# One fused two-layer kernel: modulation work respread over the merge, small chains moved under the projections, scores negated

## What is computed

```python
# block 1
h = rms_norm(x, norm_gain);  proj = h @ w_in
q, kv_all, g_nsa, br_gate, u_lru, g_lru, merge_g = split(proj)
#   NSA mixer: compress_blocks(kv) -> kc, vc (31 blocks);  softmax(q @ kc + bias) @ vc,
#   plus two causal attentions (q @ k + bias, softmax, @ v), gated and summed
#   RG-LRU mixer: causal conv of u, two block-diagonal sigmoid gates, a linear scan over time
m = sigmoid(gate_a) * (y_a @ w_proj_a) + sigmoid(gate_b) * (y_b @ w_proj_b)
x = x + m @ w_out
# block 2, its start
mod = c @ w_ada + b_ada                        # c: 1024 numbers, w_ada: 1024 x 6144
shift1, scale1, gate1, shift2, scale2, gate2 = split(mod)
h = rmsnorm(x) * (1 + scale1) + shift1         # and so on: mLSTM, differential attention, 32 experts
def compress_blocks(kv, pe, w1, b1, w2): return silu(blocks(kv, pe) @ w1 + b1) @ w2
```

## Time and profile before

| | |
|---|---|
| median of 3 runs | 1457.43 us (1455.88 to 1460.79) |
| the profiled execution: its time | 1454.09 us |
| its span, first to last instruction | 1452.2 us |
| PE busy | 1285.8 us (89%) |
| DVE busy | 519.4 us (36%) |
| ACT busy | 311.1 us (21%) |
| POOL busy | 148.4 us (10%) |
| mean granted clock of TensorE | 0.936 |
| DMA | 208.73 MB |

### The profile page before, as it was taken

The page is one execution under the profiler, slowest core; times in us unless marked ns, Lnnn a source line. Parts: engine busy times, 40 slices in busy tenths (PEclk is TensorE's granted clock), DMA queues, the critical chain, the costliest instruction groups (busy, mean ns, idle before and its releaser), DMA issues.

```text
span 1452.2 us, 12168 instructions
## 1 busy us (share of the span) xinstructions
PE 1285.8 (89%) x4480; PEld 612.9 (42%) x4480; DVE 519.4 (36%) x1391; ACT 311.1 (21%) x729; POOL 148.4 (10%) x150
## 2 busy tenths in 40 slices
PE   7998879999958899999999986999999779777774
PEld 3454334445523344664444444444444533222221
DVE  2015483667377612222722357110103333222221
ACT  3111643333200001222322343200001211111110
POOL 6000023344200000000000000000000012111101
PEclk9999999999979999999989997999999769899897
DMA  9413321332275212331310110014123659999982
GB/s 307 92 58 66 116 81 36 117 116 88 87 249 185 87 41 76 116 116 60 114 58 0 59 58 1 0 58 174 58 93 143 269 196 372 410 410 408 405 332 34
DMA packets 90815, 208.73 MB, mean 144 GB/s; under 512 B 19913, under 2 KB 50905, under 8 KB 78423
## 3 DMA queue, kind: packets, MB, share of 16 engines
q1 hardware_dynamic: 77344, 186.79, 35.0%
q0 software_dynamic: 10064, 17.96, 5.0%
q10 hardware_dynamic: 3344, 3.16, 0.7%
HBM read 203.60 MB, written 12.66 MB: 149 GB/s over the span
## 4 chain that ended last, share of the span: by engine, by line
PE 65%; DVE 13%; DMA 11%; ACT 4%; issue 3%; SPq 2%; POOL 1%; DVEq 0%; ACTq 0%; POOLq 0%
DMA AN<-in_w_up 8%; PE PS L1993 8%; PE PS L1408 8%; PE PS L1508 6%; PE PS L932 5%; PE PS L2337 5%; PE PS L2003 4%; PE PS L1553 4%; DVE AN L1205 4%; PE PS L588 3%; PE PS L1332 3%; SPq L2251 2%; PE PS L1520 2%; PE PS L1791 2%; PE PS L658 2%
## 5 line engine op out<-in xcount | busy, mean ns | idle before, releaser
L932 PE MATMUL PS<-HT,W 128*128 128x512 f32 x256 | 128.6, 627 | 3.5 <-ACT AN L1096 3.2
L1993 PE MATMUL PS<-HT,W 128*128 128x512 f32 x256 | 113.7, 597 | 0.0
L2337 PE MATMUL PS<-AN,HT 128*64 128x512 f32 x272 | 99.0, 716 | 14.6 <-DMA AN<-in_w_up 14.6
L1408 PE MATMUL PS<-W,AN 128*128 128x512 f32 x256 | 111.0, 592 | 0.9 <-DVE AN L2039 0.9
L2337 PE MATMUL PS<-W,HT 128*64 128x512 f32 x240 | 83.6, 656 | 27.0 <-DMA AN<-in_w_up 16.6
L1191 POOL TENSOR_SCALAR AN<-AN,SM 128x128 f32<-128x128 f32 (+3 forms) x64 | 71.8, 1131 | 186.1 <-DVE SM L1276 186.1
L1508 PE MATMUL PS<-W,HT 128*128 128x512 f32 x192 | 87.0, 612 | 0.0
L1205 DVE SCALAR_TENSOR_TENSOR AN<-AN,COLA 128x256 f32<-128x256 f32 x168 | 84.0, 500 | 5.8
L2286 POOL DMA_INDIRECT AN<-scr_xn,SM x16 | 16.6, 1040 | 616.4 <-DVE SM L2163 609.3
L1993 PEld LDWEIGHTS PS<-HT,W 128*128 128x128 f32 x256 | 49.1, 192 | 61.6 <-issue 61.6
L1408 PEld LDWEIGHTS PS<-W,AN 128*128 128x128 f32 x256 | 48.2, 190 | 60.5 <-issue 58.8
(11 more groups left out here) (434 smaller groups left out, 1694.2 us busy)
## 6 DMA issues: line engine op xcount, KB each, us to landing
W<-in_w_in SPq DMA_DIRECT2D x14, 2048.0 KB, 7.9
AN<-in_w_ada SPq DMA_DIRECT2D x17, 1024.0 KB, 5.2
AN<-in_w_gate SPq DMA_DIRECT2D x17, 1024.0 KB, 21.2
AN<-in_w_up SPq DMA_DIRECT2D x17, 1024.0 KB, 29.7
W<-in_w_gate SPq DMA_DIRECT2D x15, 1024.0 KB, 19.8
W<-in_w_up SPq DMA_DIRECT2D x15, 1024.0 KB, 29.7
AN<-in_w_down SPq DMA_DIRECT2D x12, 1024.0 KB, 18.5
W<-in_w_down SPq DMA_DIRECT2D x10, 1024.0 KB, 16.9
```

Source lines behind the costliest of these rows:

```text
L932: t = pe.matmul(u.ap, w[:, c, tile(m)], hT[:, c, :], start=c == 0, stop=c == 7)
L1408: t = pe.matmul(u.ap, src[:, c, tile(i)], wv(slots[n], 8, 512)[:, c, :], start=c == 0, stop=c == 7)
L1993: t = pe.matmul(u.ap, w[:, c, tile(mh)], hT[:, c, :], start=c == 0, stop=c == 7)
L2337: t = pe.matmul(u.ap[r, :].rearrange("p (n f) -> p n f", n=2), XGT[e % 2][:, c, r], w_gu(3 * e + half)[:, c], start=c == 0, stop=c == 7)
```

## The change

Four things are changed; no arithmetic is added or taken away but the negations.

1. **Modulation in the merge.** The 34 half parts are spread over merge steps 0 to 27 (`ada_step`), where each of steps 0 to 16 had two. The PE sums take banks 6 and 7 in turn, and three sum buffers are used, so a part's first chunk waits for the sum of three parts ago.
2. **Modulation in attention.** A part is done by 2 chunks in each of 4 steps (it was 4 chunks in each of 2 steps), and its load is issued as two halves of 512 KB by POOL. Its PE sum and its read-out come later.
3. **Start-up.** The raw keys' and values' transposes (`pe_blocks`), `dve_st`, the scalar chains and the clearing move up behind the bias stage, under the `q` projection; the compression is cut into three pieces, which stand between the tiles of the `u` projection; weights of `kw` and `u` swap slots 2 and 3, so that the loads of `gn` can start earlier; `kcT` goes ahead of the gates. In attention steps 0 to 3 the LRU's ACT work goes behind the score exponential.
4. **Negated scores.** Queries are scaled by -0.125 and the bias table is negated, the maximum becomes a minimum, and ACT's exponential has scale -1.0 with the minimum itself as bias. The negation L1256 falls away (64 times).

The core of the diff:

```diff
@@ act_bias
-            act.activation(B2[:, 2 * j:2 * j + 2, :].rearrange("p h k -> p (h k)"), u.ap, ACT.Copy).then_inc(*u.read)
+            act.activation(B2[:, 2 * j:2 * j + 2, :].rearrange("p h k -> p (h k)"), u.ap, ACT.Copy, scale=-1.0).then_inc(*u.read)
@@ sp_kvq
-        sp.dma_start(wv(2, 8, 280)[:, :, 0:256], wsrc(w1in, 1024, 256)).then_inc(*ring[2].up("kw"))
...
-        sp.dma_start(wv(3, 8, 512), wsrc(w1in, 1816, 512)).then_inc(*ring[3].up("u"))
+        sp.dma_start(wv(3, 8, 280)[:, :, 0:256], wsrc(w1in, 1024, 256)).then_inc(*ring[3].up("kw"))
...
+        sp.dma_start(wv(2, 8, 512), wsrc(w1in, 1816, 512)).then_inc(*ring[2].up("u"))
@@ pe_gates
+        u = B.take(0, 8, "kcT")
+        wp.wait_ge(*u.free)
+        wp.wait_ge(*cmp_dve.at("kcn"))
+        pe.transpose(u.ap[:, 0:31], KCN[0:31, :], ident[0:31, 0:31]).then_inc(*u.filled)
         for m in range(4):
@@ sp_attention
-        ws.wait_ge(*B.use("u", 3).full)
+        ws.wait_ge(*B.use("kw", 3).full)
...
-        ws.wait_ge(*B.use("cmp", 1).full)
+        ws.wait_ge(*B.use("hid").full)
@@ pe_ada
-        a = ACC[p % 2]
-        u = B.take(6, 7, "ada", p)
+        a = ada_sum(p)
+        u = B.take(6, 7, "ada", p) if p < ATT_PARTS else B.take(6, 8, "ada", p)
@@ pe_attention
-            if p is not None and r == 3:
-                pe_ada(pe, wp, p)
+            if r == 2 and 0 < p <= ATT_PARTS:
+                pe_ada(pe, wp, p - 1)
@@ act_attention
-            act_lru(act, wa, step)
+            if step >= 4:
+                act_lru(act, wa, step)
...
-                wa.wait_ge(*max_dve.at("neg", step))
-                act.activation(PU[step % 5][:, 0:n], b.ap[:, 0:n], ACT.Exp, bias=MXA[:, 2 * step + 1:2 * step + 2],
+                wa.wait_ge(*max_dve.at("max", step))
+                act.activation(PU[step % 5][:, 0:n], b.ap[:, 0:n], ACT.Exp, bias=MXA[:, 2 * step:2 * step + 1], scale=-1.0,
                                accum_out=SMA[:, step:step + 1]).then_inc(*b.read)
+            if step < 4:
+                act_lru(act, wa, step)
@@ pool_attention
+            p, half = divmod(step - 34, 4)
+            if 0 <= p < ATT_PARTS and half in (0, 2):
+                wg.wait_ge(*(ada_dve.at(p - 1, 3 + 2 * half) if p else lru_dve.at("y", 3)))
+                pool.dma_start(STAGE[0].rearrange("p (c n) -> p c n", c=8)[:, 2 * half:2 * half + 4],
+                               wada[:, 2 * half:2 * half + 4, 256 * PARTS[p]:256 * PARTS[p] + 256]).then_inc(*part_in[half // 2].up(p))
@@ dve_ada
+    def ada_sum(p):
+        return ACC[p % 2] if p < ATT_PARTS else (ACC + [TY[:, 0:256]])[p % 3]
+
+    def dve_ada(dve, wd, p, lo, hi):
...
+        for c in range(lo, hi):
+            if c % 4 == 0:
+                wd.wait_ge(*(part_in[c // 4].at(p) if p < ATT_PARTS else stage_in[s].at(p)))
             if c == 0:
-                wd.wait_ge(*(part_in.at(p) if p < ATT_PARTS else stage_in[s].at(p)))
-                wd.wait_ge(*(B.use("ada", p - 2).full if p > 1 else av_pe.at(12)))
+                if p < 2:
+                    wd.wait_ge(*av_pe.at(12))
+                elif p == 8:
+                    wd.wait_ge(*B.use("acc", 3).full)
+                else:
+                    wd.wait_ge(*B.use("ada", p - 2 if p < 8 else p - 3).full)
@@ dve_attention
-            if p is not None and r < 2:
-                dve_ada(dve, wd, p, r)
-            if p is not None and r == 3:
-                dve_mod(dve, wd, p)
+            if r == 3 and 0 < p <= ATT_PARTS:
+                dve_mod(dve, wd, p - 1)
+            if 0 <= p < ATT_PARTS:
+                dve_ada(dve, wd, p, 2 * r, 2 * r + 2)
...
                 dve.tensor_tensor_reduce(b.ap[:, lo:n], b.ap[:, lo:n], B2[:, h, 256 - (n - lo):256], 1.0,
-                                         m2 if lo else -3e38, ALU.add, ALU.max, mx).then_inc(*max_dve.up("max", step))
-                wd.wait_ge(*max_dve.at("max", step))
-                dve.tensor_scalar(m2, mx, -1.0, None, ALU.mult).then_inc(*max_dve.up("neg", step))
+                                         m2 if lo else 3e38, ALU.add, ALU.min, mx).then_inc(*max_dve.up("max", step))
@@ merge
+    def ada_step(p, half):
+
+        return (2 * (p - ATT_PARTS) + half) * 14 // (24 - ATT_PARTS)
+
     def pe_merge1(pe, wp):
         for step in range(3, 32):
             if step not in (4, 5):
                 pe_merge1_part(pe, wp, step)
-            if step < 20:
-                pe_ada(pe, wp, ATT_PARTS + step - 3)
+            for p in range(ATT_PARTS, 24):
+                if step == ada_step(p, 1) + 3:
+                    pe_ada(pe, wp, p)
@@ dve_merge1
-            if 3 <= step < 20:
-                dve_mod(dve, wd, ATT_PARTS + step - 3)
-            if step < 17:
+            for p in range(ATT_PARTS, 24):
+                if step == ada_step(p, 1) + 4:
+                    dve_mod(dve, wd, p)
+            for p in range(ATT_PARTS, 24):
                 for half in range(2):
-                    dve_ada(dve, wd, ATT_PARTS + step, half)
+                    if step == ada_step(p, half):
+                        dve_ada(dve, wd, p, 4 * half, 4 * half + 4)
@@ tensor_program
         pe_bias(pe, wp)
+        pe_blocks(pe, wp)
         pe_tokens(pe, wp, "q", 1, 512)
-        pe_tokens(pe, wp, "kw", 2, 280)
-        pe_u(pe, wp)
+        pe_tokens(pe, wp, "kw", 3, 280)
+        pe_hidden(pe, wp)
+        pe_u(pe, wp, (0,))
+        pe_turn_hidden(pe, wp)
+        pe_u(pe, wp, (1,))
+        pe_cmp(pe, wp)
+        pe_u(pe, wp, (2, 3))
         pe_turns(pe, wp)
-        pe_cmp(pe, wp)
@@ scalar_program
         act_bias(act, wa)
+        act_scalars(act, wa)
         act_q(act, wa)
         act_headnorm(act, wa)
-        act_u(act, wa)
+        act_hidden(act, wa)
+        act_u(act, wa, (0,))
+        act_turn_hidden(act, wa)
+        act_u(act, wa, (1,))
+        act_cmp(act, wa)
+        act_u(act, wa, (2, 3))
         act_turns(act, wa)
-        act_cmp(act, wa)
         act_gates(act, wa)
-        act_scalars(act, wa)
@@ vector_program
         dve_cols(dve, wd)
+        dve_st(dve, wd)
+        dve_scalars(dve, wd)
+        dve_clear(dve, wd)
         dve_headnorm(dve, wd)
-        dve_conv(dve, wd)
-        dve_st(dve, wd)
+        dve_conv(dve, wd, (0,))
+        dve_conv(dve, wd, (1,))
         dve_cmp(dve, wd)
-        dve_scalars(dve, wd)
+        dve_conv(dve, wd, (2, 3))
```

More of the change, by code:

```diff
@@ L386, in build @@
     mod_out, mod_back = sig("mod_out", "mod_back", step=16)
-    part_in, b1_in = sig("ada_part_in", "b1_in", step=16)
+    part_in = sig("ada_half0_in", "ada_half1_in", step=16)
+    b1_in = sig("b1_in", step=16)
     stage_in = sig(*[f"stage{i}_in" for i in range(4)], step=16)
@@ L650, in pool_bd, with pe_u, act_u @@
                 pool.dma_start(BD[64 * q:64 * q + 64, n, :, 64 * q:64 * q + 64], v[q]).then_inc(*bd_in.up())
-    def pe_u(pe, wp):
-        for m in range(4):
+    def pe_u(pe, wp, ms):
+        for m in ms:
             u = B.take(0, 8, "u", m)
             wp.wait_ge(*u.free)
-            wp.wait_ge(*ring[3].at("u"))
+            wp.wait_ge(*ring[2].at("u"))
             for c in range(8):
-                t = pe.matmul(u.ap, wv(3, 8, 512)[:, c, tile(m)], hT[:, c, :], start=c == 0, stop=c == 7)
+                t = pe.matmul(u.ap, wv(2, 8, 512)[:, c, tile(m)], hT[:, c, :], start=c == 0, stop=c == 7)
             t.then_inc(*u.filled)
-    def act_u(act, wa):
-        for m in range(4):
+    def act_u(act, wa, ms):
+        for m in ms:
             u = B.use("u", m)
@@ L674, in dve_conv @@
             dve.memset(RAWU[n][:, 0:3], 0.0).then_inc(*conv_dve.up("zero", n))
-        for m in range(4):
+    def dve_conv(dve, wd, ms):
+        cw, cbias = ca["conv_w"], ca["conv_b"]
+        for m in ms:
             u = RAWU[m % 2]
@@ L713, in dve_st @@
     def dve_st(dve, wd):
-        wd.wait_ge(*hn_dve.at("sum", 1))
+        wd.wait_ge(*B.use("cols").out)
         for kk in range(2):
@@ L743, in pool_b1, with pe_hidden @@
     def pool_b1(pool, wg):
-        wg.wait_ge(*hn_dve.at("sum", 1))
+        wg.wait_ge(*B.use("cols").full)
         pool.dma_start(B1R, A["cmp_b1"].rearrange("k (a n) -> a (k n)", a=1)).then_inc(*b1_in.up())
-    def pe_cmp(pe, wp):
+    def pe_hidden(pe, wp):
         u = B.take(0, 8, "hid")
@@ L816, in pe_gates @@
                 pe.matmul(u.ap, BD[:, n, m, :], UC[:, m, :], start=True, stop=True).then_inc(*u.filled)
-        u = B.take(0, 8, "kcT")
-        wp.wait_ge(*u.free)
-        wp.wait_ge(*cmp_dve.at("kcn"))
-        pe.transpose(u.ap[:, 0:31], KCN[0:31, :], ident[0:31, 0:31]).then_inc(*u.filled)
     def act_gates(act, wa):
+        u = B.use("kcT")
+        wa.wait_ge(*u.full)
+        act.activation(KCT, u.ap[:, 0:31], ACT.Identity, scale=ca["kg"][:, 0:1]).then_inc(*u.read)
         for m in range(4):
@@ L831, in act_gates @@
         act.activation(sg, sg, ACT.Sigmoid).then_inc(*gate_act.up("sg"))
-        u = B.use("kcT")
-        wa.wait_ge(*u.full)
```

(11 more changed lines are left out.)

42 lines of the change are left out of this document (19 added, 23 removed).

## The result

The changed kernel takes 1404.23 us (median of 4 runs, 1398.08 to 1407.93) where the kernel before took 1459.11 on the same chip (4 runs, 1455.88 to 1461.55): a ratio of 0.962, 95% interval 0.958 to 0.967. Measured again on another chip it took 1404.65 (6 runs, 1398.37 to 1412.64) against 1454.82 (11 runs): 0.967, 0.964 to 0.970. The forecast was 1407, range 1393 to 1423. The profiled execution of the changed kernel took 1398.08 us, 56.0 less than that of before.

The account below looks back on a forecast made before the run. PE was taken to bound the kernel, with DVE setting the merge's pace; 31 + 7.1 + 7.2 + 2.0 + 1.5 = 48.8 us gave 1405.3 from the profile, 1408.6 by the median; predicted 1407, range 1393 to 1423.

Parts of the forecast that it names:

- Merge: Merge: spreading halves over 28 steps, with two banks and three sums, lets PE set the pace; gain 31 us, bounds 13 to 37.
- DVE drops below PE: Merge steps: DVE would need 3.1 us a step against PE's 3.9, where DVE had set the pace at 5.6.
- The wait at the start: Merge steps 4 and 5: PE stands some 4.5 us until DVE has done part 7 and both halves of part 8.
- The 1.7 of lower clock: Behind the wait at the merge's start: one loss of 1.7 us, PE running matmuls at the lower clock level.
- The handshake: Merge: PE and DVE wait for each other once per part; rival: half of 25.6 us stays, total 1420, chance 0.08.
- Start-up: Before attention: work moved under projections removes 5.6 us of idle PE, faster hidden layer 1.5; gain 7.1 us.
- First attention steps: Attention up to step 4: first exponential 2.9 us after PE's start, step 4 at 8.6 instead of 15.8; gain 7.2 us.
- Negation: Attention steps 4 to 16, where DVE sets the pace: 13 units at 0.18 us each, taken as 2.0 us gain.
- Attention's modulation: Attention from 262.0 to 401.7 us: spread chunks and half loads cut PE's idle and low-clock time; gain 1.5 us of possible 5.7.
- The rival of half loads that stall: Attention: 14 half loads each stall DVE, losing from 3.5 us a stall on, at worst 1492 us; chance 0.03.
- Table loads: ACT: two more table switches, 1.28 us each by the trace, next instruction 0.01 us later; by the skill's 2.66, total 1.4 longer.
- Behind `pe_out1`: All stages behind the merge start from buffers and banks PE frees, so they only shift; no gain forecast.

Follow-up runs that it names:

- e4_readout_first: Changed kernel with DVE reading finished modulation parts out ahead of the merge step's two combinations; merge 115.27 us, whole kernel 1408.58 us.
- e8_negation_back: Changed kernel with DVE's maximum and its negation as before; 1409.59 us, single run.
- e9_scalars_late: Changed kernel with the scalar chains of ACT and DVE back ahead of attention; 1414.39 us, single run.
- e6_whole_loads: Changed kernel with attention's modulation as before: whole loads, 4 chunks in each of two steps; 1409.07 us, single run.

## Why the prediction was right

The mechanisms held: each part of the change earned time where the forecast had put it, and each part that was undone gave back time in its own stretch. That the sum came out so close was in part luck: 47.8 us were saved before `pe_out1` in the profiled pair where 48.8 were forecast, but the merge saved 3 us less than its term and attention behind step 4 some 3 us more. In order:

- **Merge, 31 forecast, 27 to 28 measured.** Two steps of the sum were off. PE's sums were taken at 14 us and were busy for 15.5 (5.6 + 5.1 + 4.8). And "DVE drops below PE" was taken to mean that no read-out is late; but a read-out stands on DVE behind combinations that wait for PE, and at the merge's end that made a new wait of 1.95 us, which e4_readout_first removed alone. The wait at the start (4.55 for 4.5 us) was right. The 1.7 of lower clock behind it was met in the first profile by luck; over the nine profiles with this wait it was 1.5 to 2.9. The forecast's other figure for the merge, 112 us from lambda's matmul, is a microsecond below its own sum (144.3 - 31) and 4 to 5 below the measured 116.3 and 117.3.
- **The handshake** was rightly named: it comes back with one bank and two sums (129.0). The forecast had not shared its gain out; spreading, bank and sum need each other.
- **Start-up, 7.1 forecast, 7.4 measured.** Idle PE time of the earlier trace rows and the slow hidden layer of the earlier trace rows account for it; undoing the compression's place alone costs 6.1. The moved chains cost nothing under `q`: no gap from 58.37 to 149.26.
- **First attention steps, 7.2 forecast, 6.7 measured.** The scalar chain was the cause. That the order inside the step carries part of it was wrong by size: 0.24 us.
- **Negation, 2.0 forecast, 3.7 to 3.8 measured.** The row's 0.18 us a unit was the distance to the negation's start, not what the next instruction loses, which is 0.245; and it counts beyond step 16 (e8_negation_back).
- **Attention's modulation, 1.5 forecast, 2.3 measured.** DVE's waits for whole loads were 9.4 us, of which the forecast had seen the first. The rival of half loads that stall has no row: none of them is waited for. Negation and spreading together, 6.1 us, and one short time at the lower clock less (1.6 us) make 7.7 where 6.6 were measured (7.0 less the 0.4 behind) and 3.5 forecast; the two effects overlap in part.
- **Table loads.** The row's 1.28 and 0.01 us hold in each run: in e9_scalars_late the load at 154.82 ends at 156.10 and its instruction starts at 156.11. The Trainium skill (page "ScalarE: Activation LUTs", section "What ACT_TABLE_LOAD costs") gives 2.66 us for a switch. The traces disagree: in all fourteen, wherever the instruction behind a load waits for nothing else, it starts 1.29 us after the load's start.
- **Behind `pe_out1`, 0 forecast, 8.1 in the profiled pair.** Its code is the same, and over fourteen profiles it took 896.2 to 911.4 us; before's 906.5 and after's 898.4 lie inside. It goes in the main with the granted clock of that part: 0.933 in the shortest, 0.915 in the longest, 0.929 in after, 0.922 in before. A profile of the changed kernel's code there with before's clock of 0.922, e6_whole_loads, took 904.8. So I count most of these 8 us as scatter and not as the change's. By medians of most runs the whole gain is 50.2 us (1454.82 - 1404.65); the 54.9 and 56.0 of the first pair hold a part of that scatter. Whether the change has some small effect there stays open.

## What to carry to other kernels

Two engines that hand one buffer to and fro need two cures: more buffers without spreading leave the slower engine's pace (125.7), spreading without them leaves the wait (129.0), both gave 117. When work is spread, look where its read-out stands in the consumer's order: behind an instruction that waits for the producer it makes a wait of its own (1.95 us here, gone once the read-out stood first). And when a change is worth 1 to 5 us in a time that varies by 15, compare the stretch between two marks of the bottleneck engine, and with it the clock and the idle time of that engine there. Identical code varied by 2.9 us from step 4 to step 20, with the clock, while its idle time stayed at 6.0.
